# The memory's keys and values ahead of x's second chunk, in the first stage of a hybrid decoder block

## The chip, the cores and the metric

The kernel runs on one core of one Trainium2 chip. A time is the device time of one execution in microseconds (us). The engines are TensorE (PE, matmuls), VectorE (DVE), ScalarE (ACT), GpSimd (POOL) and SyncE (SP, which only issues DMAs here); each works through its own instructions in order and waits on semaphores.

## The reference

One layer of a decoder block on x (2048 tokens x 1024), with a memory of 256 tokens:

```python
h = rms_norm(x, norm_g[layer])
proj = h @ w_in[layer]                      # 1024 x 7680: inputs of three branches, and their gates
y = s5_ssm(u_ssm, ...)                      # branch 1, then gelu, a gated linear unit, silu gate
o_attn = dilated_window_attention(q, k, v, ...)   # branch 2, three head groups
kv_mem = rms_norm(mem, mem_norm_g[layer]) @ w_mem_kv[layer]
...                                         # branch 3: 4 heads of q_mem attend to kv_mem
merged = (gates[:, :, 0] * (o_ssm @ w_br_ssm[layer])
          + gates[:, :, 1] * (o_attn @ w_br_attn[layer])
          + gates[:, :, 2] * (o_mem @ w_br_mem[layer]))
x = x + merged @ w_out[layer]
return rms_norm(x, final_norm_g)
```

The change is in the first stage alone: the two rms_norm, kv_mem, and the first two of the 60 tiles of `proj`.

## The kernel before

All is float32. A matmul operand is split in two: `hi` (the value rounded to fp32r) and `lo` (the rest), and a product is three passes (hi x hi, lo x hi, hi x lo; `three_pass`, lines 137 to 139). The hidden width of 1024 is 8 slices of 128.

**Jobs.** x comes in four chunks of 512 tokens, the memory is one job of 256. `jobs` has them in the order in which they are normalised: before, chunk 0, chunk 1, memory, chunk 2, chunk 3. A job j passes these steps:

- Its rows come untransposed in pieces of 256 tokens (1 MB each, `pieces`, into the two halves of `xn`); ACT squares and sums them (`squares`, four instructions of 1024 columns for a chunk, two for the memory) and takes the root (`root`).
- DVE turns that into a diagonal matrix (`normalised`), PE multiplies ones by it, which spreads the factor over the partitions (`spread`, bank<-diag,ones).
- The transposed job, loaded separately (2 MB for a chunk: `xa` or `xb`, which is a view of `ev`; 1 MB for the memory, `mem_room`), is scaled by DVE (`scaled_parts`, eight instructions), rounded by ACT to `h_hi` (`hi_parts`, two halves), and DVE computes `h_lo` (`low_parts`, two halves). Each half of h_lo counts one on `h_ready`.

**Weights.** A tile of `w_in` is 128 columns, in slot 0 or 1 of `w_raw`; DVE splits it (`split_pair`: a CAST, line 129, and a subtraction, line 131). The memory's weights `w_kv` come as four pairs of such tiles and are split into halves of h_hi and h_lo that x's later chunks do not need yet (`split_kv`).

**PE's order** in the first stage is written out by hand: 48 matmuls of ones by ones (`warm`, no use but to keep PE busy), `spread(0)`, 56 more of them, `first_tiles(0, 0)`, `spread(1)`, `first_tiles(1, 0)`, and so on. `first_tiles(s, c)` is tile s of `w_in` for chunk c: 24 matmuls of 512 columns. `memory_kv(n)` is pair n of the keys and values: 48 matmuls of 256 columns. ACT copies each pair out (`keep_kv`). After `first_tiles(1, 3)` a loop over tiles 2 to 59 runs through the rest (`project`), and later stages hang on that.

**Loads.** SP issues x's chunks 0 and 1, the memory and all weights; POOL issues pieces 2 to 8; ACT issues the transposed chunks 2 and 3 (`load_x`), at the place in its program where their buffer comes free. SP's own order is that of its program, so a wait in it holds all loads behind it.

Of the kernel before, what the change touches and what calls it, by code (L numbers as in the profile page):

```python
# [62 lines left out]
def build_program(nc, x_t, mem_t, x_n, mem_n, norm_g, mem_norm_g, final_g, w_in, w_kv, b_gate, ssm_par, ssm_d, w_glu, b_glu,  # L63
                  w_br, w_out, rel_bias, buckets, ident_c, anti_c, sign_c, steps_c, powers_c, y_out):
    ctx = ExitStack()
    with ctx:
# [239 lines left out]
        with ExitStack() as ph:  # L306
# [189 lines left out]
        xbuf = (xa, xb, mb, xa, xb)  # L496
# [38 lines left out]
        with nc.Block() as block:  # L535
            @block.sync
            def _(sp):
# [4 lines left out]
                for p in range(2):  # L542
                    sp.dma_start(xn[:, p, :, :], pieces[p]).then_inc(xn_loaded[p], 16)
# [347 lines left out]
            def _(pool):  # L891
# [129 lines left out]
            def _(act):  # L1021
# [3 lines left out]
                def squares(j):  # L1025
                    for i, p in enumerate(JOB_PIECES[j]):
                        if p < 2:
                            act.wait_ge(xn_loaded[p], 16)
                        else:
                            act.wait_ge(zs_loaded[p % 2], 16 * (p // 2))  # L1030
# [305 lines left out]
            def _(dve):  # L1336
# [3 lines left out]
                def normalised(j):  # L1340
# [5 lines left out]
                    nc.vector.tensor_tensor(diag[:, j % 2, 0:n, :], ident[:, :].unsqueeze(1).to_broadcast((P, n, P)),  # L1346
                                            r.unsqueeze(2).to_broadcast((P, n, P)), ALU.mult).then_inc(rstd_done, 1)

                def scaled_parts(j):
                    w, gi = jobs[j][0], jobs[j][4]  # L1350
                    dve.wait_ge(*((x_loaded[0], 16), (x_loaded[1], 16), (yr_loaded[3], 16), (x_loaded[0], 32),
# [9 lines left out]
                    low_parts(j)  # L1361
# [1058 lines left out]
```

## Time and profile before

| | us |
|---|---|
| median of 3 runs | 2489.52 (2488.93 to 2490.27) |
| the profiled execution | 2488.43 |
| its span | 2486.6 |
| PE busy (12570 matmuls) | 2463.2, 99% |
| DVE busy | 1396.6, 56% |
| ACT busy | 586.9, 24% |
| POOL busy | 196.5, 8% |
| granted PE clock, mean | 0.998 of full speed |

A timeline row has the start in us from the span's start, the busy time, engine, line, operation, output and inputs, shape and count; in brackets the idle time of the engine before it and what ended it. A fp32 matmul of PE may be recorded as two. In 2, the page's forty slices of 62 us, PE shows 8 tenths in the first and last and 9 in all others, and the clock 9 (full) in all. The chain of work that ended last is PE for 94% of the span.

### The profile page before, as it was taken

To read this page: it belongs to the slowest core of one execution; us is meant where nothing else is said; L and a number is where in the kernel's file an instruction comes from. 1 tells how busy PE (TensorE), PEld (TensorE's weight loads), DVE (VectorE), ACT (ScalarE), POOL (GpSimd) and SP (SyncE) were. 2 spreads that over 40 slices of the span, in tenths; PEclk is the share of its full clock that TensorE was granted. 3 is DMA by queue.
4 is the path that set the end of the run, shared out by engine and by line. 5 is a ranking of instruction groups with operands and counts; after the bars stand their busy time and mean duration, and the time that the engine had idled before them with its cause. 6 is when DMAs were issued, how large, how long until landed. Compare 5 with 4: busy or idle time off the path is not lost.

```text
span 2486.6 us, 31673 instructions
## 1 busy us (share of the span) xinstructions
PE 2463.2 (99%) x12570; PEld 2005.6 (81%) x12570; DVE 1396.6 (56%) x2591; ACT 586.9 (24%) x1262; POOL 196.5 (8%) x339
## 2 busy tenths in 40 slices
PE   8999999999999999999999999999999999999998
PEld 7888888888877777787777787888888888888887
DVE  5555776775734444413444443344435778787785
ACT  5212212222211111112333343323251111010201
POOL 0000000000001111110000000011100000100000
PEclk9999999999999999999999999999999999999999
DMA  9323334334344444441323343467665765857571
GB/s 353 110 81 98 92 103 121 109 109 125 94 134 146 149 153 154 160 146 60 125 91 113 120 148 127 141 209 244 213 218 182 264 181 169 252 171 245 159 231 60
DMA packets 172392, 382.85 MB, mean 154 GB/s; under 512 B 27088, under 2 KB 71220, under 8 KB 165077
## 3 DMA queue, kind: packets, MB, share of 16 engines
q1 hardware_dynamic: 133972, 228.74, 29.9%
q0 software_dynamic: 36192, 147.90, 17.5%
q10 hardware_dynamic: 2080, 4.19, 0.5%
q8 instruction: 100, 1.64, 0.3%
q14 instruction: 48, 0.39, 0.1%
HBM read 249.30 MB, written 131.43 MB: 153 GB/s over the span
## 4 chain that ended last, share of the span: by engine, by line
PE 94%; DVE 2%; DMA 2%; ACT 1%; issue 0%; SPq 0%; POOL 0%; DVEq 0%; ACTq 0%
PE bank L137 28%; PE bank L139 27%; PE bank L138 27%; PE bank L2128 2%; PE bank L2092 1%; PE bank L2149 1%; PE bank L2171 1%; PE bank L2107 1%; PE bank L2046 1%; PE bank L2049 1%; PE bank L2032 1%; DMA xa<-x_t 1%; PE bank L2159 1%; DMA w_raw<-w_kv 1%; ACT tsc L1130 0%; PE bank L2010 0%
## 5 line engine op out<-in xcount | busy, mean ns | idle before, releaser
L137 PE MATMUL bank<-h_hi,w_hi 128*128 128x512 f32 (+1 forms) x2720 | 1083.5, 398 | 6.1 <-DVE h_lo L1368 5.7
L139 PE MATMUL bank<-h_hi,w_lo 128*128 128x512 f32 (+1 forms) x2720 | 1057.6, 389 | 0.0
L138 PE MATMUL bank<-h_lo,w_hi 128*128 128x512 f32 (+1 forms) x2720 | 1057.4, 389 | 0.0
L137 PEld LDWEIGHTS bank<-h_hi,w_hi 128*128 128x128 f32 x2720 | 511.3, 188 | 123.2 <-issue 16.6
L139 PEld LDWEIGHTS bank<-h_hi,w_lo 128*128 128x128 f32 x2720 | 511.0, 188 | 108.1
L138 PEld LDWEIGHTS bank<-h_lo,w_hi 128*128 128x128 f32 x2720 | 511.6, 188 | 102.9 <-issue 1.4
L129 DVE CAST w_hi<-w_raw 128x1024 fp32r<-128x1024 f32 (+1 forms) x122 | 84.0, 689 | 318.5 <-PE bank L139 292.5
L137 PE MATMUL bank<-h_hi 128*128 128x512 f32 (+1 forms) x464 | 172.8, 372 | 3.1 <-issue 2.0
L139 PE MATMUL bank<-h_hi,h_lo 128*128 128x512 f32 (+1 forms) x464 | 170.4, 367 | 0.0
L138 PE MATMUL bank<-h_lo,h_hi 128*128 128x512 f32 (+1 forms) x464 | 170.3, 367 | 0.0
L907 POOL DMA_DIRECT2D proj_d<-ev x160 | 88.9, 555 | 938.3 <-ACT ev L1090 572.0
L1648 DVE COPY ptr<-bank 128x512 f32<-128x512 f32 x80 | 51.5, 686 | 184.4 <-PE bank L2128 178.2
L131 DVE TENSOR_TENSOR w_lo<-w_raw,w_hi 128x1024 fp32r<-128x1024 f32 (+1 forms) x122 | 147.9, 1212 | 4.2
L1092 ACT ACTIVATE ev<-bank 128x512 f32<-128x512 f32 x112 | 66.4, 599 | 353.9 <-PE bank L139 343.6
L1085 ACT ACTIVATE ev<-bank 128x512 f32<-128x512 f32 x64 | 38.3, 599 | 380.4 <-PE bank L139 380.4
L1130 ACT ACTIVATE tsc<-tsc,stat 128x256 f32<-128x256 f32 (+1 forms) x192 | 89.0, 464 | 126.8 <-DVE stat L1640 126.6
L137 PEld LDWEIGHTS bank<-h_hi 128*128 128x128 f32 x464 | 87.5, 189 | 20.1 <-issue 6.0
L1308 ACT ACTIVATE h_hi<-tb 128x512 fp32r<-128x512 f32 x32 | 20.2, 632 | 342.7 <-DVE tb L1860 342.7
L1579 DVE TENSOR_TENSOR tv<-bank,csb 128x512 f32<-128x512 f32 x48 | 30.9, 686 | 123.8 <-PE bank L2032 123.8
L138 PEld LDWEIGHTS bank<-h_lo,h_hi 128*128 128x128 f32 x464 | 87.5, 189 | 15.3 <-issue 1.2
L139 PEld LDWEIGHTS bank<-h_hi,h_lo 128*128 128x128 f32 x464 | 87.5, 189 | 14.5
L1090 ACT ACTIVATE ev<-bank,bgh 128x512 f32<-128x512 f32 x96 | 65.6, 684 | 107.6 <-PE bank L139 107.6
(235 smaller groups left out, 2216.9 us busy)
## 6 DMA issues: line engine op xcount, KB each, us to landing
proj_d<-ev POOLq DMA_DIRECT2D x160, 256.0 KB, 2.8
w_raw<-w_in SPq DMA_DIRECT2D x68, 512.0 KB, 5.0
gt<-proj_d POOLq DMA_DIRECT2D x32, 768.0 KB, 7.7
proj_d<-ev POOLq DMA_DIRECT2D x22, 1024.0 KB, 4.8
w_raw<-w_br SPq DMA_DIRECT2D x32, 512.0 KB, 4.4
wx_raw<-w_br SPq DMA_DIRECT2D x32, 512.0 KB, 4.3
o_d<-ev POOLq DMA_DIRECT2D x12, 1024.0 KB, 5.7
ev<-o_d SPq DMA_DIRECT2D x12, 768.0 KB, 4.3
```

The lines of the kernel that those rows point to most:

```text
L129: nc.vector.tensor_copy(hi, raw[:, s, 0:kt, :]).then_inc(w_hi_done, 1)
L131: nc.vector.tensor_tensor(lo, raw[:, s, 0:kt, :], hi.bitcast(F32), ALU.subtract).then_inc(w_split[s], 1)
L137: nc.tensor.matmul(out, ah, bh, start=(start and n == 0), stop=False)
L138: nc.tensor.matmul(out, ah, bl, start=False, stop=False)
L139: last = nc.tensor.matmul(out, al, bh, start=False, stop=(stop and n == len(pairs) - 1))
L907: pool.dma_start(dst, ring[:, e % 4, :]).then_inc(chunk_stored[e % 4], 16)
L1085: ins = nc.scalar.activation(dst, src, ACT.Silu)
L1090: ins = nc.scalar.activation(dst, src, ACT.Tanh, bias=bgh[:, t:t + 1], scale=0.5)
L1092: ins = nc.scalar.activation(dst, src, ACT.Copy)
L1130: nc.scalar.activation(e, e, ACT.Exp, bias=stat[:, 0, at:at + 1], scale=-1.0, accum_out=stat[:, 1, at:at + 1]).then_inc(e_done, 1)
L1648: nc.vector.tensor_copy(turned_rows[:, :, part, :], psum[5 + part][:, :].rearrange("p (j c) -> p j c", j=8)).then_inc(t_out, 1)
L2128: mm = nc.tensor.matmul(out, va[:, kb, HD * half:HD * (half + 1)], e, start=(part == parts[0]), stop=(part == parts[-1]))
```

## The change

The jobs are now in the order chunk 0, memory, chunk 1, chunk 2, chunk 3. With it:

- PE: 64 instead of 56 fillers behind spread(0), 8 new fillers behind first_tiles(1, 0), and all four memory_kv (with spread(2) behind the first) ahead of first_tiles(0, 1).
- SP issues all pieces, POOL none. Pair 1 and 3 of w_kv go into a buffer of their own, kv_raw (two tiles in one DMA of 1 MB), instead of w_raw. Chunk 2 is loaded by SP, chunk 3 still by ACT.
- DVE and ACT: the steps of the jobs are in a new order; low_parts no longer follows scaled_parts of itself.
- diag has one buffer instead of two; numbers of loads on semaphores follow.

PE's program in the first stage, before. The rows between are matmuls of the same group, left out; a row with `bank<-diag,ones` is a spread, `bank<-h_hi,w_hi` the first matmul of a tile (or of its second half), `bank<-h_hi` of a pair of keys and values:

```order
L1940 MATMUL bank<-diag,ones 128x512 [waits rstd_done]
L1933 MATMUL bank<-ones 128x128 x56
L137 MATMUL bank<-h_hi,w_hi 128x512 [waits h_ready,w_split0]
...
L1940 MATMUL bank<-diag,ones 128x512 [waits rstd_done]
L137 MATMUL bank<-h_hi,w_hi 128x512 [waits h_ready,w_split1]
...
L1940 MATMUL bank<-diag,ones 128x256 [waits scaled,rstd_done]
L137 MATMUL bank<-h_hi,w_hi 128x512 [waits h_ready,w_split0]
...
L137 MATMUL bank<-h_hi,w_hi 128x512 [waits h_ready,w_split1]
...
L1940 MATMUL bank<-diag,ones 128x512 [waits scaled,rstd_done]
L137 MATMUL bank<-h_hi 128x256 [waits h_ready,w_split1,w_split0]
...
L137 MATMUL bank<-h_hi 128x256 [waits h_ready,w_split1,w_split0]
...
L1940 MATMUL bank<-diag,ones 128x512 [waits scaled,rstd_done]
```
And of the change. The memory's two halves (`bank<-h_hi`) stand where the tiles of chunk 1 stood:

```order
L1964 MATMUL bank<-diag,ones 128x512 [waits rstd_done]
L1957 MATMUL bank<-ones 128x128 x64
L137 MATMUL bank<-h_hi,w_hi 128x512 [waits h_ready,w_split0]
...
L1964 MATMUL bank<-diag,ones 128x256 [waits rstd_done]
L137 MATMUL bank<-h_hi,w_hi 128x512 [waits h_ready,w_split1]
...
L1957 MATMUL bank<-ones 128x128 x8
L137 MATMUL bank<-h_hi 128x256 [waits h_ready,w_split1,w_split0]
...
L1964 MATMUL bank<-diag,ones 128x512 [waits scaled,rstd_done]
L137 MATMUL bank<-h_hi 128x256 [waits h_ready,w_split1,w_split0]
...
L137 MATMUL bank<-h_hi 128x256 [waits h_ready,kv_out,w_split1,w_split0]
...
L1964 MATMUL bank<-diag,ones 128x512 [waits scaled,rstd_done]
L137 MATMUL bank<-h_hi,w_hi 128x512 [waits h_ready,w_split0]
```
What moved: the wait for the memory's h_lo and its weights comes first, and the tiles of chunk 1 behind the last pair.

ACT's program before, from the root of chunk 1 on (L1032 squares, L1040 root, L1050 h_hi, L1190 load_x, L1059 keep_kv):

```order
L1040 ACTIVATE rcol<-ss,eps 128x2 [waits f_mm,root_done]
L1190 DMA xa<-x_t 128x8x512 [waits h_ready]
L1050 ACTIVATE h_hi<-ev 128x2048 [waits scaled] x2
L1032 ACTIVATE xn,ss<-xn 128x1024 [waits zs_loaded1]
...
L1040 ACTIVATE rcol<-ss,eps 128x4 [waits f_mm,root_done]
L1190 DMA ev<-x_t 128x8x512 [waits h_ready]
L1050 ACTIVATE h_hi<-mem_room 128x1024 [waits scaled] x2
L1032 ACTIVATE xn,ss<-xn 128x1024 [waits zs_loaded1]
...
L1040 ACTIVATE rcol<-ss,eps 128x4 [waits f_mm,root_done]
L1059 ACTIVATE mem_room<-bank 128x256 [waits kv_mm]
...
L1050 ACTIVATE h_hi<-xa 128x2048 [waits kv_mm,scaled] x2
L1059 ACTIVATE mem_room<-bank 128x256 [waits kv_mm]
```
ACT's program of the change, from the keys and values of pair 0 on (L1048 squares, L1056 root, L1066 h_hi, L1206 load_x, L1075 keep_kv):

```order
L1075 ACTIVATE mem_room<-bank 128x256 [waits kv_mm]
...
L1075 ACTIVATE mem_room<-bank 128x256 [waits kv_mm]
...
L1066 ACTIVATE h_hi<-ev 128x2048 [waits scaled] x2
L1206 DMA ev<-x_t 128x8x512 [waits h_ready]
L1048 ACTIVATE xn,ss<-xn 128x1024 [waits xn_loaded1]
...
L1048 ACTIVATE xn,ss<-xn 128x1024 [waits xn_loaded0]
...
L1056 ACTIVATE rcol<-ss,eps 128x4 [waits f_mm,root_done]
L1075 ACTIVATE mem_room<-bank 128x256 [waits kv_mm]
...
L1048 ACTIVATE xn,ss<-xn 128x1024 [waits xn_loaded1]
...
L1056 ACTIVATE rcol<-ss,eps 128x4 [waits f_mm,root_done]
L1075 ACTIVATE mem_room<-bank 128x256 [waits kv_mm]
...
L1066 ACTIVATE h_hi<-xa 128x2048 [waits kv_mm,scaled] x2
```
What moved: before, both loads stand ahead of the keys and values; now load_x(4), with its wait for h_ready, stands behind h_hi of chunk 1 and ahead of the squares of chunk 2.

SP's program of the change, from x's chunk 0 on (before, the rows of xn are not on SP, and mem_room and ev come behind both tiles of w_in):

```order
L540 DMA xa<-x_t 128x4x512 x2
L545 DMA xn<-mem_n 128x2048 [waits root_done]
L540 DMA mem_room<-mem_t 128x2048
L568 DMA w_raw<-w_in 128x1024
L119 DMA w_raw<-w_kv 128x1024 [waits w_split0]
L119 DMA w_raw<-w_kv 128x1024 [waits w_split1]
L551 DMA kv_raw<-w_kv 128x2x1024
L545 DMA xn<-x_n 128x2048 [waits root_done] x2
L540 DMA ev<-x_t 128x8x512
L119 DMA w_raw<-w_kv 128x1024 [waits w_split0]
...
L551 DMA kv_raw<-w_kv 128x2x1024 [waits w_split1,w_split0]
...
L540 DMA xa<-x_t 128x8x512 [waits h_ready]
```
What moved: the pieces of x stand among the weights, behind waits for w_split0, w_split1 and root_done.

The core of the diff:

```diff
-                dve.wait_ge(loaded[s], 16 * (n + 1 if loads is None else loads))
+                dve.wait_ge(loaded[s], 16 * ((n + 1 if n < 2 else n - 1) if loads is None else loads))
...
-        jobs.insert(2, (ML, mem_t, slice(0, ML), None, 1))
-        pieces = [x_n[0], x_n[1], x_n[2], x_n[3], mem_n[0], x_n[4], x_n[5], x_n[6], x_n[7]]
-        JOB_PIECES = ((0, 1), (2, 3), (4,), (5, 6), (7, 8))
-        PIECE_DONE = (2, 4, 7, 9, 12, 15, 17, 20, 22)
-        ROOT_DONE = (5, 10, 13, 18, 23)
+        jobs.insert(1, (ML, mem_t, slice(0, ML), None, 1))
+        pieces = [x_n[0], x_n[1], mem_n[0], x_n[2], x_n[3], x_n[4], x_n[5], x_n[6], x_n[7]]
+        JOB_PIECES = ((0, 1), (2,), (3, 4), (5, 6), (7, 8))
+        PIECE_DONE = (2, 4, 7, 10, 12, 15, 17, 20, 22)
+        ROOT_DONE = (5, 8, 13, 18, 23)
         F0 = len(jobs)
-        Z0 = (16 * 4, 16 * 3)
...
-                for p in range(2):
-                    sp.dma_start(xn[:, p, :, :], pieces[p]).then_inc(xn_loaded[p], 16)
+                def load_piece(p):
+                    if p >= 2:
+                        sp.wait_ge(root_done, PIECE_DONE[p - 2])
+                    sp.dma_start(xn[:, p % 2, :, :], pieces[p]).then_inc(xn_loaded[p % 2], 16)
+
+                def load_kv_aside(n):
+                    if n > 1:
+                        for s in range(2):
+                            sp.wait_ge(w_split[s], n)
+                    sp.dma_start(kv_raw[:, :, :, :], w_kv[2 * n:2 * n + 2].rearrange("s p k c -> p s k c")).then_inc(
+                        yr_loaded[0], 16)
+
+                load_piece(0)
+                load_piece(1)
...
                 load_x(0, slice(KD // 2, KD), x_half_loaded)
+                load_piece(2)
+                load_x(1, slice(0, KD), yr_loaded[3])
                 sp.dma_start(w_raw[:, 1, :, :], w_in[TILES[1][1]]).then_inc(w_loaded[1], 16)
-                load_x(1, slice(0, KD), x_loaded[1])
-                load_x(2, slice(0, KD), yr_loaded[3])
-                for n in range(NKV):
-                    load_pair(sp, n + 1, w_kv[2 * n], w_kv[2 * n + 1])
+                load_pair(sp, 1, w_kv[0], w_kv[1])
+                load_kv_aside(1)
+                load_piece(3)
+                load_piece(4)
+                load_x(2, slice(0, KD), x_loaded[1])
+                load_pair(sp, 2, w_kv[4], w_kv[5])
+                load_kv_aside(3)
+                load_piece(5)
+                load_piece(6)
+                sp.wait_ge(h_ready, 2)
+                load_x(3, slice(0, KD), x_loaded[0])
+                load_piece(7)
+                load_piece(8)
...
-                for p in range(2, len(pieces)):
-                    pool.wait_ge(root_done, PIECE_DONE[p - 2])
-                    pool.dma_start(xn[:, p % 2, :, :], pieces[p]).then_inc(zs_loaded[p % 2], 16)
...
-                    act.wait_ge(h_ready, 2 * (j - 2))
-                    act.dma_start(xbuf[j][:, :, :], x_t[:, :, jobs[j][2]]).then_inc(x_loaded[j - 3], 16)
+                    act.wait_ge(h_ready, 2 * (j - 1))
+                    act.dma_start(xbuf[j][:, :, :], x_t[:, :, jobs[j][2]]).then_inc(x_loaded[1], 16)
...
                 squares(1)
                 root(1)
+                hi_parts(1)
                 squares(2)
                 root(2)
-                load_x(3)
-                hi_parts(1)
+                keep_kv(0)
+                keep_kv(1)
+                hi_parts(2)
+                load_x(4)
                 squares(3)
                 root(3)
-                load_x(4)
-                hi_parts(2)
+                keep_kv(2)
                 squares(4)
                 root(4)
-                keep_kv(0)
-                keep_kv(1)
-                keep_kv(2)
+                keep_kv(3)
                 hi_parts(3)
-                keep_kv(3)
                 hi_parts(4)
...
                 def split_kv(n):
                     used = (lambda s: (kv_mm, 2)) if n == 3 else None
-                    split_pair(dve, n + 1, used, into=(kv_half(h_hi, n), kv_half(h_lo, n)))
+                    into = (kv_half(h_hi, n), kv_half(h_lo, n))
+                    if n % 2:
+                        split_pair(dve, n + 1, used, into=into, raw=kv_raw, loaded=(yr_loaded[0], yr_loaded[0]),
+                                   loads=n // 2 + 1)
+                    else:
+                        split_pair(dve, n + 1, used, into=into, loads=n // 2 + 2)
 
                 split_pair(dve, 0, None, slots=(0,))
                 dve.wait_ge(const_loaded, 112)
                 nc.vector.tensor_scalar(bgh[:, :], bg[:, :], 0.5, None, ALU.mult).then_inc(consts, 1)
                 normalised(0)
                 scaled_parts(0)
+                low_parts(0)
+                split_pair(dve, 0, None, slots=(1,))
                 normalised(1)
-                split_pair(dve, 0, None, slots=(1,))
+                scaled_parts(1)
+                low_parts(1)
+                split_kv(0)
                 normalised(2)
-                scaled_parts(1)
+                split_kv(1)
+                split_kv(2)
                 scaled_parts(2)
+                split_kv(3)
+                low_parts(2)
                 normalised(3)
-                split_kv(0)
-                split_kv(1)
+                scaled_parts(3)
                 normalised(4)
-                split_kv(2)
-                split_kv(3)
-                scaled_parts(3)
+                low_parts(3)
                 scaled_parts(4)
+                low_parts(4)
...
-                warm(56)
+                warm(64)
                 first_tiles(0, 0)
                 spread(1)
                 first_tiles(1, 0)
+                warm(8)
+                memory_kv(0)
                 spread(2)
+                memory_kv(1)
+                memory_kv(2)
+                memory_kv(3)
+                spread(3)
                 first_tiles(0, 1)
                 first_tiles(1, 1)
-                spread(3)
-                memory_kv(0)
-                memory_kv(1)
                 spread(4)
-                memory_kv(2)
-                memory_kv(3)
```

## Rows read from the trace of the kernel before

**Rows 1.** Windows: length, busy PE, PEld, DVE, ACT, POOL; granted clock; DMA share; GB/s.
```profile
10.00:20.00 10.00, 10.00 (x84) 9.42 (x84) 5.50 (x9) 2.57 (x4) 0.59 (x1) 1.00 1.03 412
...
27.03:107.20 80.17, 72.11 (x393) 61.69 (x394) 58.43 (x69) 35.48 (x55) 3.19 (x6) 0.98 0.57 207
```

**Rows 2.** Timeline of PE, first stage, columns as told above.
```profile
14.31 12.67 PE L1933 MATMUL bank<-ones 128*128 128x128 f32 x112
27.03 0.47 PE L137 MATMUL bank<-h_hi,w_hi 128*128 128x512 f32 x1
...
32.57 1.02 PE L1940 MATMUL bank<-diag,ones 128*128 128x512 f32 x2
...
45.50 0.77 PE L137 MATMUL bank<-h_hi,w_hi 128*128 128x512 f32 x1 [5.37 <-DVE h_lo L1368]
...
48.20 0.46 PE L137 MATMUL bank<-h_hi,w_hi 128*128 128x512 f32 x1
...
58.30 0.68 PE L137 MATMUL bank<-h_hi 128*128 128x256 f32 x1
...
66.60 0.36 PE L137 MATMUL bank<-h_hi 128*128 128x256 f32 x1 [1.99 <-issue]
...
72.42 1.02 PE L1940 MATMUL bank<-diag,ones 128*128 128x512 f32 x2
72.88 0.68 PE L137 MATMUL bank<-h_hi 128*128 128x256 f32 x1
...
85.25 0.47 PE L137 MATMUL bank<-h_hi,w_hi 128*128 128x512 f32 x1 [0.31 <-DVE h_lo L1368]
```

**Rows 3.** Timeline of DVE, first stage.
```profile
14.59 2.72 DVE L1359 SCALAR_TENSOR_TENSOR xa<-xa,g_in,bank 128x512 f32<-128x512 f32 x4 [1.29 <-PE bank L1940]
...
21.96 2.72 DVE L1359 SCALAR_TENSOR_TENSOR xa<-xa,g_in,bank 128x512 f32<-128x512 f32 x4 [4.65 <-DMA xa<-x_t]
...
47.48 3.22 DVE L1359 SCALAR_TENSOR_TENSOR mem_room<-mem_room,g_in,bank 128x256 f32<-128x256 f32 x8
...
50.99 2.36 DVE L1368 TENSOR_TENSOR h_lo<-mem_room,h_hi 128x1024 fp32r<-128x1024 f32 x2 [0.29 <-ACT h_hi L1050]
...
53.26 0.17 DVE L1344 RECIPROCAL rcol<-rcol 128x4 f32<-128x4 f32 x1
...
54.08 0.69 DVE L129 CAST h_hi<-w_raw 128x1024 fp32r<-128x1024 f32 x1
...
55.94 0.69 DVE L129 CAST h_hi<-w_raw 128x1024 fp32r<-128x1024 f32 x1
...
82.82 4.49 DVE L1368 TENSOR_TENSOR h_lo<-xa,h_hi 128x2048 fp32r<-128x2048 f32 x2
```

**Rows 4.** Timeline of ACT, first stage.
```profile
17.35 1.91 ACT L1050 ACTIVATE h_hi<-xa 128x2048 fp32r<-128x2048 f32 x1 [6.66 <-DVE xa L1359]
...
45.01 1.04 ACT L1032 ACTIVATE xn<-xn 128x1024 f32<-128x1024 f32 x1
...
49.29 0.30 ACT L1040 ACTIVATE rcol<-ss,eps 128x4 f32<-128x4 f32 x1
...
49.30 0.55 ACTq L1190 DMA_DIRECT2D ev<-x_t  x1
...
79.23 0.66 ACT L1059 ACTIVATE mem_room<-bank 128x256 f32<-128x256 f32 x2 [5.95 <-PE bank L139]
```

**Rows 5.** DMA: issues (us to landing) at 47.4, 49.5 and 10.6; queues from 54 to 56 us.
```profile
xn<-x_n POOLq DMA_DIRECT2D x1, 1024.0 KB, 5.0
...
xn<-x_n POOLq DMA_DIRECT2D x1, 1024.0 KB, 7.5
...
xn<-x_n POOLq DMA_DIRECT2D x1, 1024.0 KB, 10.3
...
q0 software_dynamic: 81, 0.57, 68.7%
q10 hardware_dynamic: 106, 0.22, 28.2%
```

More of the change, by code:

```diff
@@ L312, in build_program @@
                 xn = sb(pn, "xn", [P, 2, 2, D])
-                diag = sb(pn, "diag", [P, 2, CW // P, P])
+                kv_raw = sb(pn, "kv_raw", [P, 2, KD, P])
+                diag = sb(pn, "diag", [P, CW // P, P])
                 ss = sb(pn, "ss", [P, 2, CW // P])
@@ L495, in build_program @@
         mb = mem_room[:, :].rearrange("p (k c) -> p k c", k=KD)
-        xbuf = (xa, xb, mb, xa, xb)
+        xbuf = (xa, mb, xb, xa, xb)
         ring = ev[:, 0, :].rearrange("p (i c) -> p i c", c=CW)
@@ L502, in build_program @@
         jobs = [(CW, x_t, slice(CW * q, CW * (q + 1)), q, 0) for q in range(NQ)]
-        jobs.insert(2, (ML, mem_t, slice(0, ML), None, 1))
-        pieces = [x_n[0], x_n[1], x_n[2], x_n[3], mem_n[0], x_n[4], x_n[5], x_n[6], x_n[7]]
-        JOB_PIECES = ((0, 1), (2, 3), (4,), (5, 6), (7, 8))
-        PIECE_DONE = (2, 4, 7, 9, 12, 15, 17, 20, 22)
-        ROOT_DONE = (5, 10, 13, 18, 23)
+        jobs.insert(1, (ML, mem_t, slice(0, ML), None, 1))
[3 more added lines that the diff above has]
+        ROOT_DONE = (5, 8, 13, 18, 23)
         F0 = len(jobs)
-        Z0 = (16 * 4, 16 * 3)
         def job_of(c):
-            return c if c < 2 else c + 1
+            return c if c == 0 else c + 1
         def mem_half(t):
@@ L1026, in squares @@
                     for i, p in enumerate(JOB_PIECES[j]):
[L1027 to L1030, printed above, removed]
+                        act.wait_ge(xn_loaded[p % 2], 16 * (p // 2 + 1))
                         for t in range(2):
@@ L1188, in load_x @@
                 def load_x(j):
-                    act.wait_ge(h_ready, 2 * (j - 2))
-                    act.dma_start(xbuf[j][:, :, :], x_t[:, :, jobs[j][2]]).then_inc(x_loaded[j - 3], 16)
+                    act.wait_ge(h_ready, 2 * (j - 1))
+                    act.dma_start(xbuf[j][:, :, :], x_t[:, :, jobs[j][2]]).then_inc(x_loaded[1], 16)
                 def gelu(c):
-                    act.wait_ge(yr_loaded[c], 16 if c < 3 else 16 + 48)
+                    act.wait_ge(yr_loaded[c], (32 + 16, 16, 16, 16 + 48)[c])
                     for part in range(len(y_parts(c))):
@@ L1345, in normalised @@
                     dve.wait_ge(rstd_done, 2 * j + 1)
-                    nc.vector.tensor_tensor(diag[:, j % 2, 0:n, :], ident[:, :].unsqueeze(1).to_broadcast((P, n, P)),
+                    nc.vector.tensor_tensor(diag[:, 0:n, :], ident[:, :].unsqueeze(1).to_broadcast((P, n, P)),
                                             r.unsqueeze(2).to_broadcast((P, n, P)), ALU.mult).then_inc(rstd_done, 1)
@@ L1350, in scaled_parts @@
                     w, gi = jobs[j][0], jobs[j][4]
-                    dve.wait_ge(*((x_loaded[0], 16), (x_loaded[1], 16), (yr_loaded[3], 16), (x_loaded[0], 32),
+                    dve.wait_ge(*((x_loaded[0], 16), (yr_loaded[3], 16), (x_loaded[1], 16), (x_loaded[0], 32),
                                   (x_loaded[1], 32))[j])
@@ L1360, in scaled_parts @@
                                                        ALU.mult, ALU.mult).then_inc(scaled, 1)
-                    low_parts(j)
                 def low_parts(j):
@@ L1776, in _ @@
                 for n in range(KS):
-                    dve.wait_ge(zs_loaded[n % 2], Z0[n % 2] + 16 * (n // 2 + 1))
+                    dve.wait_ge(zs_loaded[n % 2], 16 * (n // 2 + 1))
                     for c in range(NQ):
@@ L1780, in _ @@
                         if u == NQ * KS - 1:
-                            split_pair(dve, N_MRG, lambda s: (g_mm, NQ * KS), slots=(1,), loads=N_MRG + 1)
+                            split_pair(dve, N_MRG, lambda s: (g_mm, NQ * KS), slots=(1,), loads=N_MRG - 1)
                         dve.wait_ge(g_sig, u + 1)
@@ L1797, in _ @@
                     elif n + 2 == KS:
-                        split_pair(dve, N_MRG, lambda s: (g_mm, NQ * (n + 1)), slots=(0,), loads=N_MRG + 1)
+                        split_pair(dve, N_MRG, lambda s: (g_mm, NQ * (n + 1)), slots=(0,), loads=N_MRG - 1)
                 for i in range(5, N_FIRST):
@@ L1831, in split_next @@
                     if i % 2 == 0:
-                        split_pair(dve, N_MRG + i, used, loads=N_MRG + i // 2 + 1)
+                        split_pair(dve, N_MRG + i, used, loads=N_MRG + i // 2 - 1)
                     else:
@@ L1940, in spread @@
                     nc.tensor.matmul(psum[SUM_BANK[j]][:, 0:w], ones[:, :],
-                                     diag[:, j % 2, 0:w // P, :].rearrange("p n c -> p (n c)"),
+                                     diag[:, 0:w // P, :].rearrange("p n c -> p (n c)"),
                                      start=True, stop=True).then_inc(f_mm, 1)
@@ L1946, in memory_kv @@
                         pe.wait_ge(w_split[s], n + 2)
-                    pe.wait_ge(h_ready, 6)
+                    pe.wait_ge(h_ready, 4)
                     if n >= 2:
```

## The prediction

> **What bounds the kernel now.** I read the busy shares first: TensorE (PE) is busy for 2463 of 2486.6 us, so a change can only move the time where PE waits or works in vain. The windows view gives the place: from 27.03, PE's first useful matmul, to 107.20, the end of the first stage, PE is busy for 72.1 of 80.2 us [rows 1]; behind it the profile's slices show nine tenths and full clock all the way. The change touches nothing behind 107. So the question is one number: when does the first stage end. PE's timeline says it [rows 2]: the filler matmuls start at 14.31, chunk 0's first tile at 27.03; then come a wait of 5.37 us in front of chunk 1's tiles, which ends at 45.50; six matmuls at the lower clock, up to 48.20 (the first lasts 0.77 us, against 0.47 at 27.03); a wait of 1.99 us in front of the second block of keys and values (66.60); and 0.31 us at 85.25, where the tiles of chunk 2 start. From 85.25 PE has four tiles without a wait, to 107.0. The same four tiles end the stage in the changed kernel, so I compare **the start of tile 0 of chunk 2: 85.25 us before**. The PE stream has units that I read off the same rows: a first tile takes 5.54 us (27.03 to 32.57), a spread of 512 columns 0.46 (72.42 to 72.88), a filler matmul 12.72 / 56 = 0.227, and a block of the memory's keys and values (85.25 - 0.31 - 72.88) / 2 = 6.03.
>
> **PE's start.** The fillers behind spread(0) go from 56 to 64: 64 x 0.227 = 14.5, so the first tile starts at 14.31 + 14.5 = 28.85, that is 1.8 us later than before, provided its input is there. It is, and long before. VectorE (DVE) starts scaling x's chunk 0 at 14.59 and before sat 4.65 us for the second half of it, until 21.96 [rows 3], since the pieces that POOL loads shared the DMA engines. The change issues those pieces on SP behind x's chunk 0, so that half (1.05 MB at 412 GB/s, 2.5 us [rows 1]) should land near 16. Then the scaling ends at 19.9 and the first h_lo at 22.2 instead of 26.9. Nobody uses these 4.7 us: PE's order has a fixed count of fillers, and spread(1), which the memory needs, stands behind the tile.
>
> **The memory.** Tile (0,0) ends and spread(1) starts at 28.85 + 5.54 = 34.4. VectorE gets the sum some 0.9 us later (it started 0.28 us behind the fillers that follow spread(0) [rows 2, 3], so this is an estimate), at 35.3. From the start of the memory's scaling to the instruction behind its h_lo are 53.26 - 47.48 = 5.8 us, to 41.1. split_kv(0) is four operations, 55.94 - 54.08 = 1.86 for each slot, so 3.7: to 44.8. PE meanwhile does tile (1,0) to 40.3 and the 8 new fillers (1.8 us, hidden by this wait) to 42.1, then **waits 2.7 us** and starts memory_kv(0) at 44.8. The loads in between are no limit: w_kv's second tile waits on SP for w_split1, which now comes at about 26.3; behind it are queued kv_raw, pieces 3 and 4 and chunk 1, 5.8 MB, 14 us at 412 GB/s, so chunk 1 is there by 43.
>
> **The keys and values.** PE: memory_kv(0) to 50.9, spread(2) to 51.3, then three blocks to 69.4. VectorE, from 44.8: normalised(2) takes 54.08 - 53.26 = 0.8, split_kv(1) and split_kv(2) 7.4 (53.1), chunk 1's scaling two times 2.72 less overlap, 5.3 (58.4), split_kv(3) 3.7 (62.1, PE needs it at 63.4), low_parts(2) 4.4 (66.5) [rows 3]. No wait for PE up to 69.4.
>
> **Chunk 1's tiles.** Here the new order on ScalarE (ACT) bites. load_x(4) waits for chunk 1's h_lo, at 66.5, and squares(3) stands behind it. Its issue takes 0.55, four squares 49.29 - 45.01 = 4.3, the root 0.3 [rows 4]: 71.7. VectorE needs 0.8 for the diagonal: spread(3) starts at 72.5, so **PE waits 3.1 us** (2.6 if the DMA's issue costs ACT nothing). Then 0.46 + 11.0 for two tiles (to 83.9) and spread(4): PE is free for chunk 2's tiles at 84.4.
>
> **Chunk 2's h_lo.** hi_parts(3) now stands behind squares(4), root(4) and keep_kv(3). Piece 7 is issued on SP when piece 5 is squared, at 69.3, piece 8 at 71.4; x's chunk 3, issued by ACT at 66.5, moves beside them. A piece of this size landed 5.0 us after its issue with little beside it, 7.5 beside such a chunk, and 10.3 in the crowd of the start [rows 5]. Piece 7 then lands at 74.3 to 76.8 and piece 8 2.5 to 3.5 us behind it, 76.8 to 80.3. I take 78.4, by the row of 54 to 56 us, where the pieces' queue moved 0.57 MB and the chunk's 0.22 [rows 5]: 0.3 MB/us, 3.5 us for each from 71. From that landing: two squares 2.1, root 0.3, keep_kv(3) 0.7, the rounding of half a chunk 1.9 [rows 4], h_lo of it 2.25 [rows 3], 7.3 in all and 0.1 for the hand-overs: 85.8. That is later than PE's own 84.4, so **PE waits 1.4 us** and starts chunk 2 at 85.8, against 85.25. The second half (88.0) and chunk 3 (95.6 against a need at 96.7) are in time.
>
> The Trainium skill (DMA: Bandwidth & Descriptors, Queues, rings and completion order) says that a DMA engine takes turns between queues packet by packet. Taken strictly, with packets of 8 KB against 2 KB, the pieces would have four fifths of the bandwidth, piece 8 would land 0.6 us earlier and the stage would end 0.6 us earlier; the row has 81 packets against 106, so turns are roughly but not strictly even, and the sum above goes by the row.
>
> **Sum.** Before: 27.03 + 58.2 = 85.25. After: +1.8 (start), -5.4 and -1.3 (wait and low clock at 45), -2.0, -0.3, and some 0.9 of small waits at spread(1), +1.8 (new fillers), +2.7, +3.1, +1.4 (new waits): some +1, and the walk of starts, which I trust more, gives +0.5. The profiled run took 2488.43 us, 1.1 below the median 2489.52; carried over to the median: 2489.52 + 0.5 = **2490.0 us**.
>
> **The other queues.** SP's weight loads for tile 2 and 3 come behind piece 8, at 71.4 or later, and are wanted only near 102. POOL loses seven loads and has nothing else until 102. Diagonal and kv_raw only change room. The numbers of loads on w_loaded and zs_loaded are bookkeeping. I cost all this at nothing; the cover is the 30 us up to 102.
>
> **Rivals.**
> 1. *Late pieces, slower.* Everything from 71 to 86 hangs on piece 8, at 1 us for 1 us once it lands after 77.0. If it takes 10.3 us from its issue at 71.4 it lands at 81.7, tile (0,2) starts at 89.1, +3.8: 2493.4. To cross 0.2% it would have to land after 82.9, or this together with a clock loss. For it: the whole chunk 3 is beside it. Against: no third stream is.
> 2. *The clock, slower.* The wait before spread(3), 3.1 us, and the one before memory_kv(0), 2.7, may each drop PE to 1.2 GHz, as the wait of 5.37 did; the one of 1.99 did not. Price: (48.20 - 45.50) - 6 x 0.227 = 1.3 us each, though what is lost at the first may be hidden by VectorE's chain: 2491.3 to 2492.7.
> 3. *The gain arrives, faster.* If VectorE and ScalarE were never last behind 28.85, PE would need 5.54 + 0.23 + 5.54 + 1.8 + 24.1 + 0.46 + 0.46 + 11.0 + 0.46 = 49.6 us and start chunk 2 at 78.5: -6.8, 2482.7. Against it stands the memory's chain of 10.4 us behind spread(1), against 7.5 us of work on PE, and four squares behind a load that waits.
> 4. *It does nothing at all*, since the gain of 4.7 us in chunk 0 is spent on fillers: this is my forecast's own mechanism, to within a microsecond.
>
> **Chances.** Forecast (2488.3 to 2491.2) 0.61; rival 1, 0.15; rival 2, 0.13; rival 3, 0.06; 0.05 for something unseen and slower. A measurement of this kernel tells about 0.2%, 5 us, from no change. Rival 1 crosses it with a third of its chance, the unseen with all of its 0.05. So: faster 0.06, same 0.84, slower 0.10. The low end: no sharing (85.25 becomes 84.4), no issue time (-0.5) and 0.6 of scatter: 2487.5. The high end takes in rivals 1 and 2: 2494.0.
>
> **What would show it.** PE's first tile at 28.9; a wait of about 2.7 us ending at 44.8 with VectorE's h_lo from w_raw as releaser; none in front of the other three blocks; a wait of about 3 us ending at 72.5 in front of spread(3), with ScalarE's squares at 67 behind it; tile (0,2) at 85.8, held by VectorE's h_lo; stage end at 107.6. If chunk 0's second half lands after 22 the start is wrong; if VectorE starts on the memory much before 35, the order on PE was misread; if the first tile of chunk 2 starts before 84, the pieces were no limit.

## The result, and the profile after

| | before | changed |
|---|---|---|
| median | 2490.12 us (11 runs, 2488.59 to 2491.78) | 2496.43 us (11 runs, 2492.95 to 2498.23) |
| profiled execution, its span | 2488.43, 2486.6 | 2498.23, 2496.4 |
| mean granted PE clock | 0.998 | 0.996 |

The ratio is 1.0026, with a 95% interval of 1.0018 to 1.0034: the changed kernel is slower, by 6.3 us. I had forecast 2490.0, no measurable change, in a range up to 2494.0. The time lies above that range. The two profiled executions lie at opposite ends: the one before is faster than all 11 runs beside it, the changed one is the slowest of its 11, so they differ by 9.8 us where the medians differ by 6.3.

PE's timeline of the changed kernel, first stage (columns as before), answers to [rows 2]:

```profile
14.99 14.45 PE L1957 MATMUL bank<-ones 128*128 128x128 f32 x128
29.20 0.48 PE L137 MATMUL bank<-h_hi,w_hi 128*128 128x512 f32 x1
...
34.76 0.60 PE L1964 MATMUL bank<-diag,ones 128*128 128x256 f32 x2
...
40.68 1.95 PE L1957 MATMUL bank<-ones 128*128 128x128 f32 x16
...
44.88 0.35 PE L137 MATMUL bank<-h_hi 128*128 128x256 f32 x1 [2.25 <-issue]
...
52.20 1.02 PE L1964 MATMUL bank<-diag,ones 128*128 128x512 f32 x2
...
73.12 2.08 PE L1964 MATMUL bank<-diag,ones 128*128 128x512 f32 x2 [2.64 <-DVE diag L1361]
...
88.23 1.12 PE L1964 MATMUL bank<-diag,ones 128*128 128x512 f32 x2 [1.65 <-DVE diag L1361]
...
92.05 0.77 PE L137 MATMUL bank<-h_hi,w_hi 128*128 128x512 f32 x1 [2.70 <-DVE h_lo L1382]
...
96.03 0.63 PE L137 MATMUL bank<-h_hi,w_hi 128*128 128x512 f32 x1
```

The start is where it was forecast: the first tile starts at 29.20, the wait in front of the memory's keys and values is 2.25 us and ends at 44.88. The waits in front of spread(3) (2.64, to 73.12) and spread(4) (1.65, to 88.23) and the one in front of chunk 2's first tile (2.70, to 92.05) follow. That tile starts 6.8 us later than before (85.25 in [rows 2]). And from 92.05 to 96.46 matmuls take 0.63 us where they take 0.39 at full clock, ten from start to start 4.41 us against 2.27: 2.1 us more. Together 8.9 us. VectorE's next CAST into w_hi, which waits for the last tile but one of the stage, stands at 110.90, before at 101.93: 9.0 us, out of 9.8 by which the two profiled executions differ. From here on I call this CAST **the mark**. From the mark to the end of the span are 2384.4 to 2386.0 us in all twelve kernels of this document, so what a kernel gains or loses stands ahead of it.

The windows view (length, busy PE, PEld, DVE, ACT, POOL, granted clock, DMA share, GB/s) shows the clock; [rows 1] had 0.98 for the whole stage:

```profile
70.00:80.00 10.00, 7.36 (x27) 5.26 (x26) 5.57 (x10) 2.64 (x7) 0.00 (x0) 0.83 0.99 348
...
90.00:100.00 10.00, 7.95 (x26) 6.39 (x27) 10.00 (x11) 3.89 (x3) 0.00 (x0) 0.67 0.00 0
```

ACT's timeline of the changed kernel from chunk 3's load on (L1048 are the squares), which answers to [rows 4]:

```profile
66.85 0.64 ACTq L1206 DMA_DIRECT2D ev<-x_t  x1
...
67.53 1.06 ACT L1048 ACTIVATE xn<-xn 128x1024 f32<-128x1024 f32 x1 [4.26 <-DVE h_lo L1382]
...
81.86 1.06 ACT L1048 ACTIVATE xn<-xn 128x1024 f32<-128x1024 f32 x1 [9.19 <-DMA xn<-x_n]
...
84.72 1.06 ACT L1048 ACTIVATE xn<-xn 128x1024 f32<-128x1024 f32 x1 [0.67 <-DMA xn<-x_n]
```

(Pieces 7 and 8 are rows of chunk 3. Chunk 2's tiles hang on them only by the order of the program: on PE spread(4) stands ahead of those tiles, and on ACT the rounding of chunk 2 stands behind the squares of both pieces. No run here changes that order.)

The chunk's load is issued at 66.85 and the squares start at 67.53, within 0.4 us of the forecast. But ACT then sits 9.19 us for piece 7, until 81.86, and gets piece 8 at 84.72. The DMA view of the same kernel: issues with KB and us to landing, and what the queues moved (q1 is SP's, q10 ACT's), from 69 to 71 and from 75 to 77 us:

```profile
ev<-x_t ACTq DMA_DIRECT2D x1, 2048.0 KB, 16.9
...
xn<-x_n SPq DMA_DIRECT2D x1, 1024.0 KB, 12.1
...
q10 hardware_dynamic: 306, 0.63, 98.3%
...
xn<-x_n SPq DMA_DIRECT2D x1, 1024.0 KB, 12.9
...
q1 hardware_dynamic: 71, 0.57, 67.4%
...
q10 hardware_dynamic: 70, 0.14, 28.4%
```

Piece 7 was issued at 69.74 and landed 12.1 us later, piece 8 12.9 us after its issue; the longest in [rows 5] was 10.3. Up to 73.2 us ACT's queue alone moves data, so nothing of piece 7 moves for 3.5 us after its issue. From piece 8's square (84.72) to the tile (92.05) are 7.3 us, the sum that the prediction had made.

### The profile page after: what moved, and what is told of

It reads as the page before. It is cut to its first block, busy times and chain, and to the rows that moved or that the text cites. A ratio compares the mean times of both kernels' runs of the same rounds, so it can differ in the third digit from the quotient of the medians.

```text
span 2496.4 us, 31736 instructions
## 1 busy us (share of the span) xinstructions
PE 2470.7 (99%) x12602; PEld 2012.2 (81%) x12602; DVE 1395.8 (56%) x2591; ACT 585.7 (23%) x1262; POOL 192.6 (8%) x332
## 4 chain that ended last, share of the span: by engine, by line
PE 94%; DVE 2%; DMA 2%; ACT 1%; issue 0%; SPq 0%; POOL 0%; ACTq 0%; DVEq 0%
PE bank L137 28%; PE bank L139 27%; PE bank L138 27%; PE bank L2152 2%; PE bank L2116 1%; PE bank L2173 1%; PE bank L2195 1%; PE bank L2131 1%; PE bank L2070 1%; PE bank L2073 1%; PE bank L2056 1%; DMA w_raw<-w_br 1%; PE bank L1957 1%; PE bank L2183 1%; DMA xn<-x_n 1%; ACT tsc L1146 0%
```

## The experiments

All times are medians of 7 to 11 runs; the kernel before, run beside the experiments, had 2489.2 to 2489.5, that is 0.6 to 0.9 us less than beside the changed kernel, which was not run again. Differences to the changed kernel are uncertain by that much; the ratios are to the kernel before of the same batch. "Tile" is the start of chunk 2's first tile in the profiled run.

| kernel | us | ratio to before, 95% | piece 8 squared from | tile | mark |
|---|---|---|---|---|---|
| before | 2490.12 | | 57.1 | 85.3 | 101.9 |
| changed | 2496.43 | 1.0018 to 1.0034 | 84.7 | 92.1 | 110.9 |
| squares first | 2485.14 | 0.9974 to 0.9992 | 73.5 | 81.1 | 98.1 |
| chunk 3 on SP, behind the pieces | 2490.03 | 0.9995 to 1.0012 | 77.0 | 86.4 | 103.4 |
| pieces on POOL | 2494.81 | 1.0015 to 1.0033 | 83.3 | 90.6 | 107.3 |
| fillers in the waits | 2493.54 | 1.0007 to 1.0024 | 82.4 | 90.6 | 107.2 |
| 40 fillers at the start | 2492.59 | 1.0004 to 1.0021 | 81.6 | 89.0 | 107.3 |
| squares first, 36 fillers | 2482.86 | 0.9960 to 0.9981 | 69.9 | 78.3 | 95.3 |
| chunk 3 in quarters | 2492.56 | 1.0004 to 1.0022 | 79.4 | 88.1 | 105.1 |
| chunk 3 in halves | 2490.32 | 0.9995 to 1.0013 | 79.7 | 87.8 | 104.9 |
| squares first, 36 and 17 fillers | 2482.99 | 0.9965 to 0.9984 | 68.7 | 77.3 | 94.3 |
| the same, quarters | 2482.91 | 0.9966 to 0.9984 | 68.9 | 77.1 | 94.1 |

**1. The squares ahead of the load that waits.** In the changed kernel ACT waits for chunk 1's h_lo only to issue chunk 3's load, and the squares of chunk 2 stand behind it.

```diff
                 hi_parts(2)
-                load_x(4)
                 squares(3)
                 root(3)
+                load_x(4)
                 keep_kv(2)
```

> Changed kernel, with ACT's squares(3) and root(3) ahead of load_x(4). Theory A (the changed kernel loses because piece 8, the last load that chunk 2's tiles hang on, lands at 84.7 us behind chunk 3's load, and each us of it goes to the end): pieces 7 and 8 are issued near 65.5 and 67.7, ahead of chunk 3's load; piece 8 lands by 74, no wait of PE over 0.5 us behind 70; chunk 2's tile starts near 82 instead of 92.05 and the stage ends near 104: 2486 to 2488. Theory B (the three stretches at the lower clock, 13.7 us in the profile, are the loss, and the pieces would not matter): only the stretch at 90 goes, 2493 to 2494. Theory C (memory first is slow in itself, by the memory's chain on VectorE): the waits move elsewhere, 2493 to 2496.

Measured: 2485.14, 11.3 us below the changed kernel, 4.1 below before in the same batch and 0.9 below the range of theory A. ACT's timeline of this kernel:

```profile
61.66 1.06 ACT L1048 ACTIVATE xn<-xn 128x1024 f32<-128x1024 f32 x1
...
66.47 0.64 ACTq L1206 DMA_DIRECT2D ev<-x_t  x1
...
70.64 1.06 ACT L1048 ACTIVATE xn<-xn 128x1024 f32<-128x1024 f32 x1 [2.82 <-DMA xn<-x_n]
...
73.54 1.06 ACT L1048 ACTIVATE xn<-xn 128x1024 f32<-128x1024 f32 x1 [0.70 <-DMA xn<-x_n]
```

The squares start at 61.66 instead of 67.53, pieces 7 and 8 are issued from 63.87 on, ahead of chunk 3's load at 66.47, and are there at 70.6 and 73.5. Behind 45 us PE has no wait, and the clock is full throughout. Theory A holds, and theory C, that memory first is slow in itself, falls: with this one line moved, the same order is faster than before. (The edit changes two things, when ACT squares chunk 2 and which load comes first. The next one parts them.)

**2. The collision alone.** Chunk 3's load goes to SP, behind piece 8; ACT still waits at the same place.

```diff
                 load_piece(8)
+                sp.wait_ge(h_ready, 6)
+                load_x(4, slice(0, KD), x_loaded[1])
...
                 hi_parts(2)
-                load_x(4)
+                act.wait_ge(h_ready, 6)
```

> Changed kernel, with chunk 3's load issued by SP behind piece 8; ACT keeps the wait for h_ready in front of squares(3) but issues nothing. It takes the collision of loads away and leaves ACT's order. Theory A: pieces 7 and 8 are issued at 69 to 71.5 as before and land near 74.5 and 77.5 instead of 81.8 and 84.7; spread(3) stays at 72.5 to 73, chunk 2's tile starts at 84.5 to 85.5 instead of 92.05: 2489 to 2491, about that of before. Theory B: the wait in front of spread(3) stays and with it its low clock: 2493 to 2494. If the late landing came from SP's queue itself and not from the load beside it, the pieces land at 80 or later and the time stays at 2496.

Measured: 2490.03, not to be told from before. The pieces' issues, then PE's spreads 3 and 4:

```profile
xn<-x_n SPq DMA_DIRECT2D x1, 1024.0 KB, 4.8
...
xn<-x_n SPq DMA_DIRECT2D x1, 1024.0 KB, 5.8
```

```profile
72.48 1.21 PE L1966 MATMUL bank<-diag,ones 128*128 128x512 f32 x2 [1.96 <-DVE diag L1363]
...
85.95 1.02 PE L1966 MATMUL bank<-diag,ones 128*128 128x512 f32 x2
```

Pieces 7 and 8, issued 0.6 us earlier than in the changed kernel (69.11 against 69.74), land after 4.8 and 5.8 us instead of 12.1 and 12.9. The wait in front of spread(3) stays (1.96 us; ACT saved the DMA's issue), and so does a slow stretch behind it: from spread(3) to spread(4) are 13.5 us here and 11.8 in experiment 1. Chunk 2's tile follows spread(4) without a wait, so the pieces are no longer last. So the collision, with the slow clock that it brings at chunk 2's tile, costs 6.4 us of the median, or 5.5 if each kernel is taken against before in its own batch: nearly all of the loss. ACT's order costs another 4.9 (against experiment 1, same batch, its slow stretch included), which the change's other savings pay.

**3. Another queue for the pieces.** POOL issues pieces 7 and 8, as before the change. (Left out: the numbers of the semaphore waits that follow.)

```diff
-                load_piece(7)
-                load_piece(8)
...
+                for p in (7, 8):
+                    pool.wait_ge(root_done, PIECE_DONE[p - 2])
+                    pool.dma_start(xn[:, p % 2, :, :], pieces[p]).then_inc(zs_loaded[p % 2], 16)
```

> Changed kernel, with pieces 7 and 8 issued by POOL (as before the change) instead of SP; chunk 3's load stays on ACT, 2.9 us ahead. If two engines' queues share fairly by packets from the issue on, and SP's queue is what held the pieces up (first packets 3.8 us after the issue), they land near 75 and 79 as I had predicted for SP: chunk 2's tile at 86.5, 2491 to 2492. If whoever comes later waits for the chunk's load whatever its queue, they land at 81 to 85 and the time stays at 2495 to 2497.

Measured: 2494.81. The issues of the pieces, and the queues from 73 to 75 us (q0 is POOL's):

```profile
xn<-x_n POOLq DMA_DIRECT2D x1, 1024.0 KB, 9.8
...
xn<-x_n POOLq DMA_DIRECT2D x1, 1024.0 KB, 10.9
...
q10 hardware_dynamic: 306, 0.62, 86.7%
...
q0 software_dynamic: 13, 0.11, 18.4%
```

POOL's pieces (issued at 70.22 and 72.30) land after 9.8 and 10.9 us, at 80.0 and 83.2, and their first packets move behind 73 us too. It is not SP's queue: on either queue the pieces wait behind the chunk's load. The 75 us at which piece 7 should have landed with fair turns is missed by 5. (The edit moves one thing more: the next weights, 1 MB on SP, no longer stand behind piece 8 and are issued at 60.78 instead of 72.19. Whether the 2 us by which the pieces land sooner than in the changed kernel come from that is not shown.)

**4. Fillers in the waits**, so that the clock stays up.

```diff
...
-                warm(8)
+                warm(17)
...
                 memory_kv(3)
+                warm(15, 1)
                 spread(3)
...
+                pe.wait_ge(scaled, 24)
+                warm(12, 2)
                 spread(4)
+                pe.wait_ge(scaled, 32)
+                warm(10, 3)
```

(The second argument is the PSUM bank.)

> Changed kernel, with filler matmuls in PE's waits: 17 instead of 8 ahead of memory_kv(0), 15 ahead of spread(3), 12 ahead of spread(4), 10 ahead of chunk 2's first tile. Each group is shorter than the wait that it fills. It takes the clock's part away and leaves every chain of loads. Theory A: chunk 2's tile still starts near 92, but at full clock; the stage ends 2.3 us earlier: 2493 to 2494.5. Theory B: 2489 to 2491. No stretch at the lower clock before 120 us by either.

Measured: 2493.54, with all 11 runs between 2493.10 and 2494.11, where the changed kernel's spread over 5.3 us. The clock is full in the whole stage. PE's last fillers:

```profile
84.87 2.84 PE L1957 MATMUL bank<-ones 128*128 128x128 f32 x24
...
87.55 1.02 PE L1964 MATMUL bank<-diag,ones 128*128 128x512 f32 x2
...
88.41 2.40 PE L1957 MATMUL bank<-ones 128*128 128x128 f32 x20
...
90.56 0.48 PE L137 MATMUL bank<-h_hi,w_hi 128*128 128x512 f32 x1
```

So fillers give back 2.9 us of the median, 2.0 if each kernel is taken against before in its own batch, and most of the scatter: three of the changed kernel's 11 runs, at 2492.95 to 2493.19, are where all runs of this one are, to within 1.2 us. The chain of loads is the rest, 3.4 to 4.3 us. The profiled runs can't make it sharper. Their marks differ by 3.7 us, of which 2.1 are the slow stretch at chunk 2's tile; the tile itself starts 1.5 us earlier, because piece 8's squares start 2.3 us earlier (82.38), and whether the fillers or chance did that is not shown. By the chain of 7.3 us the tile could even have started at 89.7; the last ten fillers overshot, and it started at 90.56.

**5. Fewer fillers at the start**, 40 for 64 (`warm(64)` becomes `warm(40)`).

> Changed kernel, with 40 instead of 64 fillers behind spread(0); nothing else. In the changed kernel chunk 0's first h_lo is there at 22.8 us and PE starts at 29.4; now PE starts at 24.0, 5.4 earlier. Theory A: the chain from spread(1) over the memory, the splits, chunk 1 and the squares shifts by 5.4 us as a whole, pieces 7 and 8 and chunk 3's load among it, so the collision stays: 5 us less than the changed kernel, 2490 to 2492. Rival: loads that do not shift (chunk 1, pieces 3 to 6, from 29 us on) become the bound, or the clock falls in a longer wait: 2493 to 2496.

Measured: 2492.59, 3.8 us less. Two lines of VectorE (the memory's scaling, and the wait for the root of chunk 1) and ACT's issue of chunk 3's load:

```profile
30.79 3.22 DVE L1374 SCALAR_TENSOR_TENSOR mem_room<-mem_room,g_in,bank 128x256 f32<-128x256 f32 x8 [2.70 <-PE bank L1964]
...
42.73 0.18 DVE L1359 RECIPROCAL rcol<-rcol 128x4 f32<-128x4 f32 x1 [2.64 <-ACT rcol L1056]
...
64.52 0.63 ACTq L1206 DMA_DIRECT2D ev<-x_t  x1
```

The memory starts 4.7 us earlier (30.79 for 35.47), but then VectorE waits 2.64 us for ACT, whose pieces 3 and 4 did not come earlier: they stand on SP behind the wait for w_split1. At chunk 3's load 2.3 us are left, at chunk 2's tile 3.1. Both theories had a part: the chain shifts, and loads that don't shift take half of it. PE's waits in front of spread(3) and of chunk 2's tile (2.70) stay, with slow stretches behind them.

**6. Both**, squares first and 36 fillers.

> squares(3) and root(3) ahead of load_x(4), and 36 fillers instead of 64. Theory A: both gains add: 6.2 us less than with the squares moved alone, which was 2485.1: 2479 to 2480, the fastest of all. The mark of the stage, VectorE's first CAST into w_hi, at 92 instead of 98.1. Rival: the first gain had already freed PE from waits, so the loads (pieces 7 and 8 at 7 us each, chunk 3's at 14) now decide and only 2 to 3 us come: 2482 to 2483.

Measured: 2482.86 (7 runs), 2.3 us less than squares first and 6.6 less than before in the same batch, the fastest with the next two. I had expected 6.2 us; the rival's 2 to 3 is what came, though by other loads than it named. PE's timeline of this kernel behind 60 us:

```profile
60.21 0.36 PE L137 MATMUL bank<-h_hi 128*128 128x256 f32 x1 [1.60 <-issue]
...
66.04 1.02 PE L1964 MATMUL bank<-diag,ones 128*128 128x512 f32 x2
...
77.83 1.02 PE L1964 MATMUL bank<-diag,ones 128*128 128x512 f32 x2
```

PE now waits 1.60 us in front of the last pair of keys and values, at 60.21, the only wait behind 40 us: VectorE's split of that pair ends at 60.1. VectorE in turn had stood still in front of chunk 1's diagonal, and ACT in front of chunk 1's squares:

```profile
41.95 0.18 DVE L1359 RECIPROCAL rcol<-rcol 128x4 f32<-128x4 f32 x1 [3.29 <-ACT rcol L1056]
```

```profile
36.95 1.06 ACT L1048 ACTIVATE xn<-xn 128x1024 f32<-128x1024 f32 x1 [3.27 <-DMA xn<-x_n]
```

So the chain is last again from the landing of chunk 1's pieces 3 and 4 on, as in experiment 5: they are issued at 27.90, in the changed kernel at 28.34, although PE starts 6 us earlier. Chunk 1's reciprocal stands at 44.69 in the changed kernel, 2.7 us later than here, and chunk 2's tile starts 2.8 us earlier than in experiment 1. Pieces 7 and 8, which the rival had named, hold nothing.

**7 and 8. The load that is in the way.** Chunk 3's load in four DMAs back to back, and in two halves, the second behind root(3). (Shown is the first; the wait for more loads is left out.)

```diff
-                    act.dma_start(xbuf[j][:, :, :], x_t[:, :, jobs[j][2]]).then_inc(x_loaded[1], 16)
+                    for i in range(4):
+                        ks = slice(2 * i, 2 * i + 2)
+                        act.dma_start(xbuf[j][:, ks, :], x_t[:, ks, jobs[j][2]]).then_inc(x_loaded[1], 16)
```

> Changed kernel, with chunk 3's load issued by ACT as four DMAs of two slices each, one behind the other; same bytes, queue and time. It asks why a later load waits until 73.5 us whatever its queue. If it is the backlog of bytes in the engines' queues, nothing changes: piece 7 lands 9.8 to 12 us after its issue, 2494 to 2497. If one DMA is handled as one lot, piece 7 gets in behind the first or second quarter and lands 2 to 3 us earlier, 2492 to 2494; squares(3) then begins up to 1.5 us later, for the three more issues on ACT.

> Changed kernel, with chunk 3's load in two halves: the first where it was, the second behind root(3), 5 us later, at 72 us and so behind the issues of pieces 7 and 8. Theory A: only 1 MB is ahead of the pieces, moved by about 71.5; piece 7 lands near 76 and piece 8 near 79, chunk 2's tile starts at 86 to 87: 2491 to 2492. If what holds the pieces up is any load ahead of them, of whatever size, they stay at 80 to 84 and the time at 2495 to 2497.

Measured: 2492.56 and 2490.32. With quarters, ACT's queue from 69 to 71 us, piece 7's issue, and SP's queue from 73 to 75:

```profile
q10 hardware_dynamic: 404, 0.78, 106.0%
...
xn<-x_n SPq DMA_DIRECT2D x1, 1024.0 KB, 6.2
...
q1 hardware_dynamic: 72, 0.59, 71.9%
```

The four parts move 0.78 MB in the two microseconds in which the single DMA moved 0.63, and piece 7 (issued at 70.77, 1 us later than in the changed kernel, for ACT's three more issues) lands after 6.2 us instead of 12.1. Still nothing of it moves before 73: the part of my second theory by which it gets in between two quarters isn't what happened. What is gone is the slow end: the single DMA of 2 MB, issued at 66.85, landed after 16.9 us although 2.0 of its 2.1 MB had moved by 77; the quarters landed after 4.0 to 6.5 us. With halves piece 7 lands after 7.1 us, as theory A said, with the tile at 87.8 against 86 to 87, and the time came out 0.7 to 1.7 us better than expected. In both kernels, as in experiment 2, the tile follows spread(4) without a wait: the pieces are no longer last. Why the single DMA dragged isn't settled; the traces have no single engine's share. That it is one DMA isn't enough for it, for in experiment 1, where it comes behind the pieces, the same single load moves as fast as the quarters (ACT's queue from 76 to 78 us):

```profile
q10 hardware_dynamic: 382, 0.78, 101.3%
```

**9 and 10. What is left.** Experiment 6 with 17 fillers in front of the first pair, and this with quarters too.

> squares(3) first, 36 fillers behind spread(0), and 17 instead of 8 ahead of memory_kv(0), whose wait of 2.25 us was followed by 3.4 us at the lower clock. Theory A: PE is not last between there and the last pair of keys and values (it waits 1.6 us for VectorE in front of it), so the 1.3 us that the clock gives back are swallowed by that wait: 2482.5 to 2483, same as without. If the clock there were on the path, 2481 to 2482.

> The same with chunk 3's load in four DMAs of two slices. Theory A: nothing waits for the pieces or for chunk 3 any more, and three more issues on ACT stand behind root(3): 2482.5 to 2483.5, no gain though the load lands faster. If piece 8 still decided when chunk 2's tiles start, up to 1 us less.

Measured: 2482.99 and 2482.91, both as theory A had it. Once the order on ACT is right, neither the clock behind the first wait nor the form of chunk 3's load moves the median. In the profiled runs the mark is a microsecond earlier (94.3 and 94.1 for 95.3), which the medians, with 4.1 to 5.5 us from lowest to highest, can't show. VectorE's wait in front of chunk 1's diagonal (3.46 us in experiment 9) is still there.

## Why the prediction was wrong

**Right, to within a microsecond.** The start at 28.85 (29.20; the first weights came 0.7 us late in this run), the wait of 2.7 that ends at 44.8 (2.25, to 44.88), the squares of chunk 2 at 67.1 (67.53), spread(3) at 72.5 after a wait of 3.1 (73.12, after 2.64), and the 7.4 us from piece 8's landing to the tile (7.3).

**The step that failed: the landing of piece 8.** I put it at 78.4, between 76.8 and 80.3, from a row of the kernel before in which the pieces' queue had 0.57 MB while the chunk's had 0.22. But there piece 7 had been issued 1.8 us ahead of the chunk (47.47 against 49.30), and piece 8 just behind it (49.55). In the changed kernel the chunk's load has 2.9 us ahead. It moved alone to 73.2 us, and the pieces landed at 81.8 and 84.6. What I had left out is who comes first. The row itself was read correctly, but only for two loads that both have packets moving. The Trainium skill (DMA: Bandwidth & Descriptors, Queues, rings and completion order) describes turns packet by packet between queues. The trace agrees from 75 to 77 us, with 71 packets against 70, and experiment 8's from 77 to 81, with 271 against 268; these are counts over all 16 engines. From 73 to 75 us they are 30 against 250, and for the 3.5 us in which piece 7 had been issued and nothing of it moved, the section has no reason. In experiment 2, with nothing ahead, piece 7's first packets moved 0.9 us after its issue.

The trace of the kernel before had the sign, in a place where I didn't look. There SP issues two weight tiles at 56.05 and 57.92, while chunk 3's load is under way. The queues from 57 to 59 us, and the second tile's landing:

```profile
q10 hardware_dynamic: 373, 0.76, 103.0%
...
w_raw<-w_kv SPq DMA_DIRECT2D x1, 512.0 KB, 6.0
```

SP's queue moves no packet before 59.5, and the tiles land after 6.6 and 6.0 us, those issued from 64.66 on after 3.1 to 4.0.

I also took landing as bytes by bandwidth. SP's queue had moved 1.52 MB by 79 us, more than piece 7 has, and piece 7, the first in it, was signalled at 81.8.

**The chances.** Rival 1 (late pieces) had its price right, 1 us for 1 us, but I capped it at 10.3 us after the issue, the worst row of before, and it was 12.9: at 84.6 it is past the 82.9 that I had named as the point for 5 us. Rival 2 (the clock) came too, and I had added it as an alternative with 0.13. They aren't alternatives: here the late pieces make the wait behind which the clock falls. Its price was too low as well: I had 1.3 us for a stretch, and the one at 92.05 cost 2.1, the one behind spread(3) 1.7 (hidden, since PE then waited for piece 8). 3.4 to 4.3 us are the loads and 2.0 to 2.9 the clock. The range had to reach for their sum, and the chance of slower, 0.10, was too small.

**The rivals that fell.** The gain of 6.8 us (rival 3) did not come with the change as it stood, but 6.6 us came with one line moved and 36 fillers. That the sizes agree is luck: rival 3 had PE without a wait behind 28.85, and experiment 6 starts 6 us earlier and still waits twice. The reason that I gave against it, four squares behind a load that waits, was the thing to try. The clock also fell after a wait of 2.25 us (at 44.88), between the 1.99 that hadn't been enough and the 5.37 that had; it can have cost nothing there, since PE waited for the squares later on.

## What to carry to other kernels

A load that nobody needs for 27 us, issued 3 us ahead of two that the program waits for next, cost 5.5 to 6.4 us here. When a change moves the issues of DMAs, write down for each not only the bytes beside it but what is ahead of it and who needs which first. An instruction that waits only to issue a DMA (here for a free buffer) belongs behind the computing that doesn't need that wait. And waits that follow from one cause come together with the clock that they cost, so their prices are to be added, not weighed against each other. Last, look in the trace before for a load that was issued into another's running transfer, and see when its first packets moved.

## What I had not expected of the hardware

- A piece of 1 MB, issued 2.9 us behind a 2 MB load of 2 KB packets, landed after 12.1 us from SP's queue, and from POOL's, 3.2 us behind, after 9.8; with nothing ahead, after 4.8. Its first packets moved 3.5 us after its issue, with nothing ahead after 0.9.
- The same 2 MB load, ahead of the pieces, moved at 0.31 MB/us as one DMA and at 0.39 as four, and its landing took 16.9 us against 4.0 to 6.5 for each of the four. As one DMA it also moved at 0.39 in experiment 1 and at 0.38 before, so the rate isn't bound to the form.
- Waits of 2.25, 2.64 and 2.70 us each had a stretch at half the clock beside or behind them in the changed kernel's profile; a wait of 2.24 us at the same place in experiment 1 had none. Of the eight profiled kernels with 2.24 or 2.25 us in front of the memory's keys and values, four (changed, 2, 5, 6) show the slow stretch and four (1, 3, 7, 8) don't. The same kernel's runs then differ by up to 5.3 us, and by 1.0 with the waits filled.
